# Six open weight blocks instead of five in the first stage of a two-layer decoder trunk

## What is computed

```
mod = silu(c) @ ada_w[0] + ada_b[0]          # 6 parts of 1024: shift, scale, gate, shift, scale, gate
h   = rms_norm(x) * gain * (1 + scale) + shift
b_g, c_g, xv = split(h @ sc_w_in[0], 3)      # three 1024x1024 products
z   = c_g * xv;  z = conv3(z)                # depthwise, causal, width 3
y   = (b_g * z) @ sc_w_out[0]
x   = x + gate * y                           # then an MLP, then an attention layer and its MLP
```

## Time and profile before

| | |
|---|---|
| median of 3 runs | 1161.05 us (1160.62 to 1161.6) |
| the profiled execution, its own time | 1160.05 us |
| its span, first to last instruction | 1158.3 us |
| busy in the span | PE 1152.1 us (99%), PEld 967.7 us, DVE 866.7 us, ACT 543.4 us, POOL 25.3 us |
| chain of work that ended last | PE 95%, DVE 2%, DMA 1%, ACT 1% |
| granted TensorE clock | 1.000 over the span |

### The profile page before, as it was taken

One profiled execution on the slowest core, in us unless ns is written; L12 is line 12 of the kernel. 1 busy time (PEld: TensorE's weight loads), 2 busy tenths in 40 slices (PEclk: granted clock), 3 DMA queues, 4 the chain that ended last, 5 costly groups with the idle time before them and its releaser, 6 DMA issues.

```text
span 1158.3 us, 16333 instructions
## 1 busy us (share of the span) xinstructions
PE 1152.1 (99%) x5839; PEld 967.7 (84%) x5839; DVE 866.7 (75%) x1191; ACT 543.4 (47%) x876; POOL 25.3 (2%) x37
## 2 busy tenths in 40 slices
PE   8999999999999999999999999999999999999999
PEld 6788889988888888888978888889988888888887
DVE  4666988975675675555889988897887778779694
ACT  5322333531331341333677887775665445445521
POOL 2000000000000000200020000000000000000000
PEclk9999999999999999999999999999999999999999
DMA  9977655476666666333255554464133323332311
GB/s 296 293 220 229 200 178 184 128 232 189 197 192 192 196 190 191 93 92 91 74 128 142 131 132 127 110 164 146 40 103 114 109 81 103 108 119 82 108 56 73
DMA packets 207324, 168.89 MB, mean 146 GB/s; under 512 B 5684, under 2 KB 180188, under 8 KB 207260
## 3 DMA queue, kind: packets, MB, share of 16 engines
q1 hardware_dynamic: 207068, 167.92, 49.2%
q10 hardware_dynamic: 160, 0.06, 0.0%
q0 software_dynamic: 32, 0.07, 0.0%
HBM read 153.24 MB, written 2.10 MB: 134 GB/s over the span
## 4 chain that ended last, share of the span: by engine, by line
PE 95%; DVE 2%; DMA 1%; ACT 1%; SPq 0%; issue 0%; DVEq 0%
PE bank L788 24%; PE bank L789 24%; PE bank L790 24%; PE bank L1102 4%; PE bank L1103 4%; PE bank L1104 4%; PE bank L1279 2%; PE bank L1261 2%; PE bank L1251 1%; PE bank L1252 1%; PE bank L970 1%; PE bank L971 1%; PE bank L973 1%; PE bank L927 1%; DMA ada_first<-in_ada_w 1%; DVE h_lo L2005 0%
## 5 line engine op out<-in xcount | busy, mean ns | idle before, releaser
L788 PE MATMUL bank<-h_hi,w_hi 128*128 128x512 f32 (+1 forms) x848 | 318.8, 376 | 0.3 <-DVE h_lo L2005 0.3
L790 PE MATMUL bank<-h_hi,w_lo 128*128 128x512 f32 (+1 forms) x848 | 316.5, 373 | 0.0
L789 PE MATMUL bank<-h_lo,w_hi 128*128 128x512 f32 (+1 forms) x848 | 316.4, 373 | 0.0
L1418 ACT ACTIVATE w_hi<-raw 128x1024 fp32r<-128x1024 f32 x149 | 156.3, 1054 | 154.4 <-DMA raw<-in_mlp_w 116.4
L1951 DVE TENSOR_TENSOR w_lo<-raw,w_hi 128x1024 fp32r<-128x1024 f32 x149 | 181.4, 1221 | 33.4 <-ACT w_hi L1418 32.5
L788 PEld LDWEIGHTS bank<-h_hi,w_hi 128*128 128x128 f32 x848 | 159.7, 188 | 29.1 <-DVE h_lo L2005 0.8
L790 PEld LDWEIGHTS bank<-h_hi,w_lo 128*128 128x128 f32 x848 | 159.7, 188 | 28.4
L789 PEld LDWEIGHTS bank<-h_lo,w_hi 128*128 128x128 f32 x848 | 159.7, 188 | 27.6 <-issue 0.2
L788 PE MATMUL bank<-g_hi,w_hi 128*128 128x512 f32 (+1 forms) x416 | 154.8, 372 | 0.0
L790 PE MATMUL bank<-g_hi,w_lo 128*128 128x512 f32 (+1 forms) x416 | 153.5, 369 | 0.0
L789 PE MATMUL bank<-g_lo,w_hi 128*128 128x512 f32 (+1 forms) x416 | 153.4, 369 | 0.0
(11 more groups left out here) (293 smaller groups left out, 1684.1 us busy)
## 6 DMA issues: line engine op xcount, KB each, us to landing
raw<-in_mlp_w SPq DMA_DIRECT2D x96, 512.0 KB, 4.0
ada_raw<-in_ada_w SPq DMA_DIRECT2D x40, 1024.0 KB, 5.6
w_raw<-in_mlp_w SPq DMA_DIRECT2D x32, 512.0 KB, 3.4
raw<-in_sc_w_in SPq DMA_DIRECT2D x18, 512.0 KB, 4.1
raw<-in_w_kv SPq DMA_DIRECT2D x16, 512.0 KB, 3.9
ada_first<-in_ada_w SPq DMA_DIRECT2D x24, 256.0 KB, 5.8
raw<-in_q_w SPq DMA_DIRECT2D x8, 512.0 KB, 4.8
keys<-qk SPq DMA_DIRECT2D x16, 256.0 KB, 3.1
```

Source lines behind the costliest of these rows:

```text
L788: mm(out[:, cols], weights_hi, hi[:, k, cols], start=(k == 0), stop=False)
L789: mm(out[:, cols], weights_hi, lo[:, k, cols], start=False, stop=False)
L790: return mm(out[:, cols], weights_lo, hi[:, k, cols], start=False, stop=(k == KT - 1))
L1418: go(w_hi[:, jj, :, :], raw[:, jj, :, :], ACT.Copy).then_inc(hi_ok, 1)
```

## The change

A sixth block is open: block 5's weights come as two-k pieces through the buffers `beside_raw`, `beside_hi` and `beside_lo`, as block 4's do through `spare_raw`, and its products for tile k stand behind those of block 4. Its bank is 7, which also serves to turn x tiles 4 and 6, so its first matmul waits for the last x tile's copy (`X_TAKEN`, `LATE_BLOCKS`). Block 6 takes weight slot 1, and block 7 takes slot 2 in two halves; its high part stands on ACT behind the fourth eviction, its low part on DVE before the second `ada_step`. Block 8's load waits for nothing more, and its low part stands before the fifth `ada_step`. The turned rows go to bank 4.

```
-FIRST_BLOCKS = GROUP + 1
-FIRST_BANK = [0, 1, 2, 3, 5]
+FIRST_BLOCKS = GROUP + 2
+FIRST_BANK = [0, 1, 2, 3, 5, 7]
-X_TAKEN = [1, 2, 3, KT - 1, KT - 2]
-SOON, LATE_BLOCKS = (0, 1, 2, 4), (3,)
+X_TAKEN = [1, 2, 3, KT - 1, KT - 2, KT]
+SOON, LATE_BLOCKS = (0, 1, 2, 4), (3, 5)
...
+                    sp.dma_start(beside_raw[:, 0, k:k + 2, :], first_w[:, k:k + 2, c0 + P:c0 + 2 * P]
+                                 ).then_inc(spare_in[k // 2] if k // 2 < KT // 2 - 1 else beside_in, 16)
...
             sp.wait_ge(first_used, 2)
-            load_block(1, c_g(GROUP + 1))
+            load_block(1, c_g(GROUP + 2))
             sp.wait_ge(ms_ok, TT)
             ada_pair(0, 0, 2, 0)
             sp.wait_ge(first_used, 3)
-            load_block(2, c_g(GROUP + 2))
+            sp.dma_start(raw[:, 2, 0:STRIPS, :], c_g(GROUP + 3)[:, 0:STRIPS, :]).then_inc(raw_in[2], 16)
             ada_pair(1, 0, 2, 1)
             sp.wait_ge(hi_ok, KT // 2)
-            sp.dma_start(beside_raw[:, 0, :, :], c_g(GROUP + 3)).then_inc(raw_in[3], 16)
+            sp.dma_start(raw[:, 2, STRIPS:, :], c_g(GROUP + 3)[:, STRIPS:, :]).then_inc(raw_in[3], 16)
             x_v = columns(sc_w_in[0], 2 * D)
-            sp.wait_ge(pe_done, FIRST_BLOCKS)
             load_block(0, x_v(0))
...
-                    sp.wait_ge(pe_done, KT + n - 3)
+                    sp.wait_ge(pe_done, KT + n - (2 if n < 3 else 3))
                     load_block(s, x_v(n))
...
-            turn(bank[7][:, 0:ROWS], rows_a[:], ident[0:ROWS, 0:ROWS]).then_inc(cols_pe, 1)
-            for jj in range(FIRST_BLOCKS - GROUP, GROUP - 1):
-                dense(1, jj, h_hi, h_lo)
-            pe.wait_ge(bank_free, GROUP)
-            part_of(KT - 1, 0, bank[GROUP - 1], h_hi, h_lo, range(KT), weights=(beside_hi, beside_lo)).then_inc(pe_done, 1)
+            turn(bank[4][:, 0:ROWS], rows_a[:], ident[0:ROWS, 0:ROWS]).then_inc(cols_pe, 1)
+            for b in range(FIRST_BLOCKS, KT):
+                pe.wait_ge(bank_free, b - 3)
+                part_of(b, b - FIRST_BLOCKS + 1, bank[b - GROUP], h_hi, h_lo, range(KT)).then_inc(pe_done, 1)
...
+            def split_first_beside(k):
+
+                if k % 2 == 0:
+                    if k // 2 == KT // 2 - 1:
+                        act.wait_ge(beside_in, 16)
+                    go(beside_hi[:, 0, k:k + 2, :], beside_raw[:, 0, k:k + 2, :], ACT.Copy).then_inc(spare_hi_ok, 1)
...
             x_tile(7)
             x_tile(6)
+            split_first_beside(0)
...
             def step_cg(g, jj, j):
                 if j == 1:
-                    split_beside()
-                if j >= FIRST_BLOCKS:
+                    split_late(2)
+                if j == GROUP:
+                    split(2, 0)
+                if j > GROUP + 1:
                     split(g, jj + 3)
                 ada_step(g, jj, j, 2)
```

More of the change, by code:

```diff
@@ L303, in yoco_trunk @@
         spare_in = [sem(f"spare_in{q}") for q in range(KT // 2 - 1)]
+        beside_in = sem("beside_in")
         spare_hi_ok = sem("spare_hi_ok")
@@ L959, in first_weights @@
                     return first_hi[:, k, b * P:(b + 1) * P], first_lo[:, k, b * P:(b + 1) * P]
-                pe.wait_ge(spare_lo_ok, k // 2 + 1)
-                return spare_hi[:, 0, k, :], spare_lo[:, 0, k, :]
+                if b == GROUP:
+                    pe.wait_ge(spare_lo_ok, k // 2 * 2 + 1)
+                    return spare_hi[:, 0, k, :], spare_lo[:, 0, k, :]
+                pe.wait_ge(spare_lo_ok, k // 2 * 2 + 2)
+                return beside_hi[:, 0, k, :], beside_lo[:, 0, k, :]
             def first_products(k, blocks=range(FIRST_BLOCKS)):
@@ L979, in opening_weights @@
             def opening_weights(b):
-                return first_hi[:, 0, b * P:(b + 1) * P] if b < GROUP else spare_hi[:, 0, 0, :]
+                if b < GROUP:
+                    return first_hi[:, 0, b * P:(b + 1) * P]
+                if b > GROUP:
+                    pe.wait_ge(spare_hi_ok, 2)
+                return (spare_hi if b == GROUP else beside_hi)[:, 0, 0, :]
             def opening_high(half):
@@ L1529, in split_first @@
                 go(first_hi[:, k, :], first_raw[:, k, :], ACT.Copy).then_inc(hi_ok if k % 2 else first_hi_ok,
-                                                                             2 if k == KT - 1 else 1)
+                                                                             3 if k == KT - 1 else 1)
                 if k % 2 == 0:
-                    act.wait_ge(*((spare_in[k // 2], 16) if k // 2 < KT // 2 - 1 else (raw_in[0], 32)))
+                    act.wait_ge(*((spare_in[k // 2], 32) if k // 2 < KT // 2 - 1 else (raw_in[0], 32)))
                     go(spare_hi[:, 0, k:k + 2, :], spare_raw[:, 0, k:k + 2, :], ACT.Copy).then_inc(spare_hi_ok, 1)
+            def split_first_beside(k):
[3 more added lines that the diff above has]
+                    go(beside_hi[:, 0, k:k + 2, :], beside_raw[:, 0, k:k + 2, :], ACT.Copy).then_inc(spare_hi_ok, 1)
             def first_tile(j):
@@ L1551, in _, with split_seventh @@
                 first_tile(k)
+                split_first_beside(k)
             split(1, 1)
-            split(1, 2)
-            def split_beside():
+            def split_seventh():
+                act.wait_ge(raw_in[2], 32)
                 act.wait_ge(raw_in[3], 32)
-                go(beside_hi[:, 0, :, :], beside_raw[:, 0, :, :], ACT.Copy).then_inc(hi_ok, 1)
+                go(w_hi[:, 2, :, :], raw[:, 2, :, :], ACT.Copy).then_inc(hi_ok, 1)
             def step_cg(g, jj, j):
@@ L1564, in step_cg @@
                    of.rearrange("p (a t) -> p a t", a=1), ACT.Copy).then_inc(bank_free, 1)
-                if j == 1:
-                    split_beside()
-                if j >= FIRST_BLOCKS:
+                if j == 3:
+                    split_seventh()
+                if j > GROUP:
                     split(g, jj + 3)
@@ L2115, in split_first @@
                 tt(first_lo[:, k, :], first_raw[:, k, :], first_hi[:, k, :],
-                   ALU.subtract).then_inc(lo_ok if k % 2 else first_lo_ok, 2 if k == KT - 1 else 1)
+                   ALU.subtract).then_inc(lo_ok if k % 2 else first_lo_ok, 3 if k == KT - 1 else 1)
             def split_first_spare(k):
                 if k % 2 == 0:
-                    dve.wait_ge(spare_hi_ok, k // 2 + 1)
+                    dve.wait_ge(spare_hi_ok, k // 2 * 2 + 1)
                     tt(spare_lo[:, 0, k:k + 2, :], spare_raw[:, 0, k:k + 2, :], spare_hi[:, 0, k:k + 2, :],
+                       ALU.subtract).then_inc(spare_lo_ok, 1)
+                    dve.wait_ge(spare_hi_ok, k // 2 * 2 + 2)
+                    tt(beside_lo[:, 0, k:k + 2, :], beside_raw[:, 0, k:k + 2, :], beside_hi[:, 0, k:k + 2, :],
                        ALU.subtract).then_inc(spare_lo_ok, 1)
@@ L2183, in _, with split_late @@
                 split_first_spare(k)
-            split(1, 1)
-            split(1, 2)
+            def split_late(s):
+                dve.wait_ge(hi_ok, FIRST_BLOCKS + s)
+                tt(w_lo[:, s, :, :], raw[:, s, :, :], w_hi[:, s, :, :], ALU.subtract).then_inc(lo_ok, 1)
+            split_late(1)
             dve.wait_ge(cols_pe, 3)
-            nc.vector.tensor_copy(cols[:, R_MLP:ROWS], bank[7][:, R_MLP:ROWS]).then_inc(cols_ok, 1)
+            nc.vector.tensor_copy(cols[:, R_MLP:ROWS], bank[4][:, R_MLP:ROWS]).then_inc(cols_ok, 1)
             dve.wait_ge(cols_ok, 3)
@@ L2206, in _ @@
             dve.wait_ge(acc_zero, 1)
-            def split_beside():
-                dve.wait_ge(hi_ok, KT)
-                tt(beside_lo[:, 0, :, :], beside_raw[:, 0, :, :], beside_hi[:, 0, :, :], ALU.subtract).then_inc(lo_ok, 1)
             def step_cg(g, jj, j):
                 if j == 1:
-                    split_beside()
-                if j >= FIRST_BLOCKS:
+                    split_late(2)
+                if j == GROUP:
+                    split(2, 0)
+                if j > GROUP + 1:
                     split(g, jj + 3)
```

## The result

| | before | changed |
|---|---|---|
| median | 1160.24 us (12 runs, 1159.72 to 1161.6) | 1162.88 us (12 runs, 1161.66 to 1164.65) |
| ratio | | 1.0021, 95% interval 1.0014 to 1.0028 |
| profiled execution | 1160.05 us, span 1158.3 us | 1162.18 us, span 1160.4 us |

The sixth open block makes the kernel 0.21% slower, 2.4 us by the ratio (1.6 to 3.2), 2.1 us between the profiled executions. The forecast was 1163.3 us: +2.2 us on the three-run median of 1161.05.

What follows compares the result with a forecast made beforehand. The prediction took PE's own pace to bound the first stage. Added products +5.5, removed block -5.44, opening +0.25 and block 9's wait +1.9 gave +2.2 us: median 1163.3 us, with an 8-in-10 range of 1161.2 to 1165.3.

Steps and rivals of the forecast that it cites:

- PE paces the stage: First stage: PE's own pace sets the 5.14 us step, so extra products fill no hole; steps become 5.8 us.
- Rival (a): First stage: the DVE and ACT chain sets the step, so extra matmuls are free; 1159.1 us; chance 0.08.
- The opening: Start of the first stage: PE waits about 0.25 us for block 5's first high part from ACT.
- the added products: First stage: block 5's three matmuls for each of eight tiles, at 0.69 us per tile, cost 5.5 us.
- Behind the turn: After the first stage: block 9's load, held in SP's queue, makes PE wait 1.9 us for its low part.
- T: Start of the turn of the small rows, ending the first stage: 55.94 us before, forecast about 61.7.
- Rival (b): Behind the turn: block 9 isn't late, its DMA overtaking or landing in 4.9 us; 1161.4 us; chance 0.14.
- Cover: Behind the turn, spare time before PE wants a block: block 7 0.9 us, block 12 about 0.8.
- rival (c): Behind the turn: more than one block is late (7, 10 or 12); 1164.4 to 1165.6 us; chance 0.17.
- Rival (d): At block 9: the wait lowers the granted clock from 2.4 to 1.2 GHz; 1168.7 us; chance 0.03.
- The sum: Whole kernel: +5.5 - 5.44 + 0.25 + 1.9 = +2.2 us, giving a median of 1163.3 us.
- the moved matmuls: 24 matmuls moved from behind the turn into the first stage: 5.5 us added, 5.44 removed, net +0.1 us.

Runs made afterwards that it cites:

- the trace with 6.9 us: Changed kernel with block 9's load moved one place later in SP's queue, behind the fifth pair of modulation rows: 1169.82 us, ratio 1.0085.
- the two versions without the wait at block 9 or 10: Changed kernel with the turn ahead of tile 7's products (1160.58 us, 1.0002); changed kernel with loads of blocks 9, 10 and 11 issued earlier (1160.32 us, 0.9999).
- the early turns: Turn moved ahead of tile 7's products: changed kernel 1160.58 us, also with block 5's first matmul behind unit 1's strips 1160.66; kernel before 1160.79.
- those with less work: Kernel before, leaving out one of block 4's three matmuls for tiles 1 to 7 (1159.75 us, 0.9995), or all for tiles 1 to 6 (1159.45, 0.9994).

## Why the prediction was right, step by step

**PE paces the stage.** Right. The stage's steps are 5.81 us (5.8 forecast). Rival (a), 1159.1 us, fell: the added matmuls are paid in full, and matmuls taken out of a step shorten it in full. The strips' weight loads take 0.109 us each and those of full width 0.188, which is why the weight-load share is lower in the stage. The Trainium skill ("Trainium Kernel Development and Optimization", Performance Expectations) names the busy share of weight loads, beside MFU (the share of the peak arithmetic rate), as a good measure of how close a kernel is to its roofline. Read as room for more matmuls, as rival (a) read it, that share misled here: three more lengthened the step by 0.67 us. (Rival (a)'s 6 x 0.69 is 4.1, not 4.2.)

**The opening.** 0.25 us forecast. From the late block 3 to the strips it takes 0.95 us now against 0.32; less one matmul of 0.23, the wait and its restart cost 0.40. From there to the turn it is 44.34 us (17.25 to 61.59), 5.80 more than before; 5.75 was forecast. So the opening was sized 0.15 too small, and the added products, with 5.40 us instead of 5.5, 0.1 too large. Taking the wait away gave back 0.16 us in one trace and nothing in the times, which the forecast did not see.

**Behind the turn.** Each time, counted from T, came as forecast: first `ada_step` T + 2.28 (2.27), fourth done T + 8.68 (8.66), block 9's load T + 9.12 (9.1), ACT T + 15.65 (15.96), low part done T + 17.97 (18.29). The load landed 6.5 us after issue instead of 6.8. So this term was sized 0.2 too large: 1.7 us of wait with its restart instead of 1.9. Rival (b), no wait, fell.

**Cover.** Blocks 7 and 8 were not waited for, and neither was block 10 (rival (c)): its low part was ready at 84.63 and PE came at 85.2, 0.6 us of cover where 0.7 was worked out. The prediction had said that block 9's wait pushes PE's demand back, and had counted the wait into block 10's cover. What it did not draw from this is that the cover is lent: take block 9's wait away, and block 10's appears. It called the wait one late load; the experiments show a late queue. For the forecast itself this made no difference.

**The clock.** Rival (d) did not happen at 1.4 us of waiting (clock 1.00 in every stretch), but it does at 6.9 (clock 0.50). The Trainium skill ("TensorE: Matmul & The Clock Gate", Part 1) says that throttled is the default and that activity releases it; the trace with 6.9 us agrees. The 3 in 100 that I gave it were right for this length only.

**The sum.** +2.2 forecast, 2.1 between the profiled executions, 2.4 by the ratio. Three small misses nearly cancel in it, the opening 0.15 too small, the products 0.1 and the wait 0.2 too large, and that is luck. So is part of the closeness of 1163.3 to 1162.88: twelve runs put the median before at 1160.24, 0.8 us under the three-run median that the forecast started from, and the two medians lie 2.6 us apart. By the two versions without the wait at block 9 or 10 (1.0002 and 0.9999), the wait is all of the loss that can be measured; the 0.4 us of the opening can be read in the traces, but it and the 0.1 us for the moved matmuls lie inside the intervals of the times, and aren't shown there.

## What to carry to other kernels

Work moved from behind a point into the work ahead of it delays all that hangs on that point; count every engine's chain from it, and ask for each load what its place is in the queue, not only when its slot is free. A late block seen in a trace can stand for several: moving one load only passed the wait to the next, moving all three, or moving the source of the delay, removed it. And more open work in a stage helps only where its steps have holes: compare starts of matmuls, not busy shares.

## What I had not expected

A wait of PE costs more than its length once it is long. At 1.4 us nothing was added but 0.1 us of restart; at 6.9 us the granted clock was 0.50 from 82 to 88 us, with PE idle from 78.2 to 85.1, which added 1.5 us. Between the two lengths no run was made. Several kernels (the early turns, and those with less work) also show a wait of 0.5 to 0.7 us of PE for `queries<-qk` some 550 us later, in the attention layer, which neither the kernel before nor the changed one has; why it comes and goes is open.
